# A diffusion-transformer trunk on one NeuronCore: the context's modulation moved from ScalarE to GpSimd

## What is computed

```python
def modulate(x, g, shift, scale):
    return rms_norm(x, g) * (1.0 + scale) + shift

for l in range(DEPTH):                       # DEPTH = 2
    need_ctx = l < DEPTH - 1
    m  = split(silu(c)     @ ada_w[l] + ada_b[l], 6)      # latent:  sh1, sc1, g1, sh2, sc2, g2
    mc = split(silu(c_ctx) @ ada_w[l] + ada_b[l], 6)      # context: csh1, csc1, ...
    h_l = modulate(x,  norm1_g[l], sh1, sc1)
    h_c = modulate(xc, norm1_g[l], csh1, csc1)
    y_c, y_l = mixer_sublayer(h_c, h_l, ...)              # attention, gated DeltaNet, pooling
    x = x + g1 * y_l
    x = x + g2 * expert_choice_ffn(modulate(x, norm2_g[l], sh2, sc2), ...)
    if need_ctx:                                          # layer 0 alone
        xc = xc + cg1 * y_c
        xc = xc + cg2 * expert_choice_ffn(modulate(xc, norm2_g[l], csh2, csc2), ...)
return x
```

## Time and profile before

| | us |
|---|---|
| median of 3 runs | 2088.85 |
| lowest, highest | 2085.29, 2117.83 |
| profiled execution, its own time | 2093.35 |
| its span, first to last instruction | 2091.5 |
| mean granted TensorE clock | 0.968 |

### The profile page before, as it was taken

One profiled execution on the slowest core, in us unless ns is written; L12 is line 12 of the kernel. 1 busy time (PEld: TensorE's weight loads), 2 busy tenths in 40 slices (PEclk: granted clock), 3 DMA queues, 4 the chain that ended last, 5 costly groups with the idle time before them and its releaser, 6 DMA issues.

```text
span 2091.5 us, 41301 instructions
## 1 busy us (share of the span) xinstructions
PE 1957.1 (94%) x17607; PEld 1274.3 (61%) x17607; DVE 725.3 (35%) x1507; ACT 597.9 (29%) x1167; POOL 363.2 (17%) x411
## 2 busy tenths in 40 slices
PE   6999989799999999899999899989889999999998
PEld 4565556678878654455556445546688885455554
DVE  3054233433443316021121325333345443523223
ACT  4111843342232404111110131383342224311111
POOL 2412000143333001211011031200135330000000
PEclk8999999899999999899999999999989999999999
DMA  9400001144444315799999612100100002479996
GB/s 322 134 28 21 21 0 34 37 140 140 160 153 144 100 41 176 232 327 332 344 347 325 241 41 61 41 0 21 51 13 13 18 7 101 161 310 409 414 408 265
DMA packets 196888, 320.65 MB, mean 153 GB/s; under 512 B 10761, under 2 KB 163119, under 8 KB 189583
## 3 DMA queue, kind: packets, MB, share of 16 engines
q1 hardware_dynamic: 184928, 287.20, 39.1%
q0 software_dynamic: 6432, 20.00, 3.5%
q10 hardware_dynamic: 5390, 11.44, 1.6%
HBM read 305.45 MB, written 13.16 MB: 152 GB/s over the span
## 4 chain that ended last, share of the span: by engine, by line
PE 50%; DVE 3%; ACT 3%; issue 2%; DMA 1%; SPq 1%; POOL 0%; DVEq 0%; ACTq 0%; POOLq 0%
PE psum L560 7%; PE psum L1029 6%; PE psum L1077 5%; PE psum L1055 5%; PE psum L1036 3%; PE psum L1140 3%; PE psum L935 3%; PE psum L1089 1%; PE psum L680 1%; PE psum L878 1%; PE psum L866 1%; PE psum L881 1%; PE psum L731 1%; PE psum L700 1%; PE psum L1164 1%
## 5 line engine op out<-in xcount | busy, mean ns | idle before, releaser
L560 PE MATMUL psum<-hT,ring 128*128 128x256 f32 (+2 forms) x976 | 338.9, 504 | 4.7 <-ACT hT L1454 4.2
L560 PEld LDWEIGHTS psum<-hT,ring 128*128 128x128 f32 (+1 forms) x976 | 184.9, 192 | 146.4 <-issue 128.7
L1029 PE MATMUL psum<-ring,arena 128*64 128x256 f32 x1024 | 125.1, 400 | 19.8 <-issue 16.0
L935 PE MATMUL psum<-hT,ring 128*128 128x512 f32 (+1 forms) x384 | 139.6, 521 | 1.1 <-DVE xT L2209 0.9
L878 PE MATMUL psum<-ring,wbuf 64*64 64x64 f32 x1920 | 124.1, 227 | 3.4 <-DVE wbuf L2174 2.8
L881 PE MATMUL psum<-wbuf,ring 64*64 64x64 f32 x1920 | 121.7, 224 | 0.0
L2481 POOL TENSOR_TENSOR mlaw<-ring,lev 128x512 f32<-128x512 f32 x72 | 91.3, 1272 | 162.2 <-PE psum L866 159.9
L1029 PEld LDWEIGHTS psum<-ring,arena 128*64 128x64 f32 x1024 | 78.0, 144 | 60.4 <-issue 29.9
L2296 DVE TENSOR_TENSOR arena<-arena,psum 128x384 f32<-128x384 f32 (+1 forms) x32 | 15.6, 487 | 284.5 <-PE psum L1036 185.4
L935 PEld LDWEIGHTS psum<-hT,ring 128*128 128x128 f32 x384 | 72.6, 190 | 65.3 <-issue 60.3
L878 PEld LDWEIGHTS psum<-ring,wbuf 64*64 64x64 f32 x1920 | 104.1, 141 | 7.0 <-issue 5.0
(11 more groups left out here) (323 smaller groups left out, 3392.8 us busy)
## 6 DMA issues: line engine op xcount, KB each, us to landing
ring<-in_moe_w_gate SPq DMA_DIRECT2D x64, 1024.0 KB, 10.2
ring<-in_ada_w SPq DMA_DIRECT2D x48, 1024.0 KB, 5.3
ring<-in_moe_w_up SPq DMA_DIRECT2D x48, 1024.0 KB, 8.1
ring<-in_moe_w_down SPq DMA_DIRECT2D x32, 1024.0 KB, 10.8
ring<-in_w_in SPq DMA_DIRECT2D x20, 1024.0 KB, 5.9
big<-in_moe_w_down SPq DMA_DIRECT2D x16, 1024.0 KB, 14.4
ring<-in_w_out SPq DMA_DIRECT2D x8, 1024.0 KB, 5.2
xT<-in_moe_w_up SPq DMA_DIRECT2D x8, 1024.0 KB
```

The lines of the kernel that those rows point to most:

```text
L560: m = pe.matmul(b[0:c1 - c0, 0:n], lhsT=w[:, k, c0:c1], rhs=hT[:, k, t0:t0 + n], start=k == 0, stop=k == KD - 1)
L935: m = pe.matmul(b[:, 0:x], lhsT=w[:, k, c:c + P], rhs=mixT[:, k, t0:t0 + x], start=k == OUT_REST[0], stop=k == OUT_GDN[-1])
L1029: m = pe.matmul(b[e * CAP_L:(e + 1) * CAP_L, 0:2 * P], lhsT=xs[:, k, e, 0:CAP_L], rhs=w[e][:, k, :], start=k == 0, stop=k == KD - 1)
```

## The change

ScalarE modulates the latent columns only and counts `h1` or `h2` up for them. The context's columns are modulated in place by GpSimd: a new function `context_norm` waits for the modulation values, then for each block for VectorE's product, and runs one 128x256 `tensor_scalar` with a multiplication and an addition, both with one value for each partition; it counts a new semaphore `hc` up. It is called behind the fill of `big` in both layers, and behind the DeltaNet in layer 0. TensorE waits for `hc` as well as for `h1` and, in layer 0, `h2`. In layer 0 `parameters(0)` now stands behind the eight operations of the first norm, and its own wait is gone.

```diff
@@ TensorE, input projection
                         if key[2] == "pool0":
                             pe.wait_ge(s["h1"], k + 1)
+                            pe.wait_ge(s["hc"], k + 1)
@@ TensorE, router
                     pe.wait_ge(s["h2"], k + 1)
+                    if need_ctx:
+                        pe.wait_ge(s["hc"], KD + k + 1)
@@ ScalarE, norm
                     act.wait_ge(s["hx%d" % which], k + 1)
-                    for g in segs:
-                        t0, n = SEGS[g]
-                        c = 1 - g
-                        m = act.activation(hT[:, k, t0:t0 + n], hT[:, k, t0:t0 + n], ACT.Identity,
-                                           bias=mods_of[l][:, (0 if which == 1 else 3) * KD + k, c:c + 1],
-                                           scale=amod_of[l][:, which - 1, k, c:c + 1])
-                    m.then_inc(s["h%d" % which], 1)
+                    act.activation(hT[:, k, CTX:T], hT[:, k, CTX:T], ACT.Identity,
+                                   bias=mods_of[l][:, (0 if which == 1 else 3) * KD + k, 0:1],
+                                   scale=amod_of[l][:, which - 1, k, 0:1]).then_inc(s["h%d" % which], 1)
@@ GpSimd
+            def context_norm(l, which):
+
+                s = sems[l]
+                pool.wait_ge(s["mods%d" % which], 1)
+                for k in range(KD):
+                    pool.wait_ge(s["hx%d" % which], k + 1)
+                    x = hT[:, k, 0:CTX]
+                    pool.tensor_scalar(x, x, amod_of[l][:, which - 1, k, 1:2],
+                                       mods_of[l][:, (0 if which == 1 else 3) * KD + k, 1:2], ALU.mult, ALU.add
+                                       ).then_inc(s["hc"], 1)
...
                 pool.memset(at(big, 0, (2 * UW,)), 0.0).then_inc(s["upad"], 1)
+                context_norm(l, 1)
                 if l == 0:
-                    evacuated(pool, ("am", ADA_FIRST - 1))
                     parameters(0)
...
+                if need_ctx:
+                    context_norm(l, 2)
                 product_ready(pool, ("rt", l))
```

More of the change, by code:

```diff
@@ L307, in build_program @@
         s_outrow = sem("s_outrow")
-        NAMES = ["zero", "zrow", "pcol", "par", "mods1", "mods2", "rinv", "sq1", "sqd1", "hx1", "h1", "sq2", "sqd2", "hx2", "h2", "upad", "pool", "sqm",
+        NAMES = ["zero", "zrow", "pcol", "par", "mods1", "mods2", "rinv", "sq1", "sqd1", "hx1", "h1", "hc", "sq2", "sqd2", "hx2", "h2", "upad", "pool", "sqm",
                  "abw", "abraw", "abexp", "abln", "gbd", "row1", "rowr", "rowa", "row2", "nm", "pv", "cv1", "qkv", "lsq",
```

## The result

The changed kernel takes **2104.2 us** (median of 22 runs, 2096.14 to 2118.42), the kernel before 2094.0 us beside it (22 runs, 2081.76 to 2117.83). The ratio is 1.0048, 95% interval 1.0032 to 1.0064: 10 us slower, between 6.7 and 13.4. That is within 2% and inside the forecast's range of 2084 to 2111 (its middle was 2094), and about twice the +5.3 us of its sum. The profiled execution took 2109.81 us with a span of 2108.0.

The account below looks back on a forecast made before the run. TensorE, busy 94% of the span, bounds the kernel. Stretches of +4.3 us and 1 for the clock on the profiled 2093.35 give 2098.7; on the median's scale 2088.85 + 5.3 = 2094 us, range 2084 to 2111.

Parts of the forecast that it names:

- The places: Three norms, both of layer 0 and the first of layer 1, hold the possible gain, the largest at layer 1.
- GpSimd's operation, 0.93 us: Each of 24 added GpSimd modulations in the norms was priced at 0.93 us from line 2414, within 0.35 to 1.85.
- The lower bound, 0.35: Lowest price of one GpSimd modulation, 0.35 us, estimated from a plain copy; the three norms would then give -3.1 us.
- the prediction's own formula for pairs: In the norms, 0.82 us for a product after release plus GpSimd's operation less 0.14 hidden: 1.61 for one k.
- The alternation: In the three norms VectorE's products and GpSimd's operations take turns, 1.61 us for one k; 2094 us, chance 0.50.
- rival B: In the norms VectorE keeps the port until all eight products end; 15 to 25 us, time 2104, chance 0.13.
- The sum by stretches: Delays of +0.2 and +1.6 us at layer 0's two norms and +2.5 at layer 1's first, +4.3 together.
- The clock, 1 us within 0 to 5.2: Clock lost through TensorE's pauses at layer 1's first norm, taken as short: 1 us, bounds 0 and 5.2.
- What was costed at nothing: Moved parameter DMAs, the later pooling chain, 24 extra TensorE waits and the load of GpSimd's code: 0 us.
- rival E: GpSimd's code load starts only when layer 0's first context columns are there; sum 12.9 us, time 2103, chance 0.07.
- D: A GpSimd operation in the norms costs 1.85 us; some 25 us at the bound, 2114, middle about 2104, chance 0.15.
- C: GpSimd's single-scalar reads don't block VectorE's products in the norms; -3.3 us, time 2085.6, chance 0.15.

Follow-up runs that it names:

- the three shares: Kernel before with one norm given to GpSimd: layer 0's second +4.2 us, layer 1's first +3.1, layer 0's first with the moved loads +1.7.
- the probe with gaps: Changed kernel plus a tail repeating VectorE products and GpSimd modulations, in this round with a wait between products; the tail adds some 75 us.
- experiment 4: Changed kernel with the inverse roots left in PSUM and each product split at 256 columns; 2087.12 us, ratio 0.9967 to the kernel before.
- experiment 8: Kernel before, ScalarE alone, with the latent columns taken first and signalled apart from the context ones; 2090.77 us, ratio 1.0000.

## Why the prediction was right, and where it was wrong

**The places.** Right as far as the runs can tell: the three shares make 9.0 of 9.4 us, with about 4 us of uncertainty on each. The ranking, layer 1's first norm (+2.5) ahead of the second of layer 0 (+1.6), stays open: the times say 3.1 and 4.2, with intervals that overlap, and the traces 3.6 and 3.0, unless the clock falls in the second norm. The first norm of layer 0 was to lose 0.2 us and lost 1.8 to 2.5.

**GpSimd's operation, 0.93 us.** Wrong: 0.55 to 0.56. The row it was taken from has one operation and costs more than the form with two. The lower bound, 0.35, was nearer. By the prediction's own formula for pairs, 0.82 + (0.56 - 0.14) = 1.24 us, and the probe with gaps shows 1.23; that part of the working holds. The Trainium skill (GPSIMD Engine Reference, Engine selection), which was set aside for the row, has one-input operations roughly line-rate; the prediction put that at its lower bound, 0.35, and the 0.55 measured is nearer to it than to 0.93.

**The alternation, the likeliest case (0.50).** Wrong for this code, and this is the step that failed. The rows it rested on the earlier trace rows show single operations meeting; there the second waits for the first. VectorE's eight products are queued back to back, a new one every 0.87 us while each lasts 0.95, and GpSimd got in only around every third: 2.67 and 2.80 us for an operation of 0.56, while the products grew by 0.20 us twice. The prediction had seen "products start every 0.87 though each lasts 0.95" and booked it under rival B, at 0.13. In its place the runs show something between the two: the second context columns come at +6.6 us, where alternation had 4.2, and the last ones at +10.55. Both cases had the last ones later, alternation at 13.25 and B at about 14.5, but only because they priced the operation at 0.93. At the measured 0.56 alternation would have had them at 1.82 + 0.42 + 6 x 1.24 + 0.56 = +10.2, ahead of the last step of today (10.79), and its sum would have been near nothing. That the forecast had the right sign was luck: the price that was too high made up for a blockade that was too mild. The Trainium skill (SBUF — State Buffer, Who interferes with whom) says that the two contend, and they do; that the second to issue waits for the whole of the first is what the probe with waits shows, not the back-to-back one, where GpSimd waits for three products.

**The sum by stretches.** +0.2, +1.6 and +2.5 were worked out from the *last* columns. What decided was an early block: TensorE's steps of 1.31 us can't catch up from the second one, at +6.78: seven of them took 9.19 us and ended at +15.97, against 804.58 - 791.59 = 12.99, so 3.0 us are lost with the clock at 2.4 GHz. At layer 1, where two products of 0.43 make a step, the last one starts at 6.78 + 6 x 0.86 = 11.9, against 1221.77 - 1210.98 = 10.79: +1.1, and +1.5 was found with the clock up.

**The clock, 1 us within 0 to 5.2.** Too small: 2.6 us where it fell in the second norm of layer 0 and about 2 at layer 1 (15.2 to 15.8 against 13.49). After TensorE's pauses of 2.6 and 1.3 us it fell in one of four traces in the second norm of layer 0, and at layer 1 in all six. "These pauses are short" came from the alternation, and went with it.

**What was costed at nothing.** Right. The parameter loads are issued by 61.4, and the pooling chain starts at 61.38, 0.7 us later than in the earlier trace rows (timeline of the changed kernel); nobody waited for it.

```profile
60.80 0.62 POOL L2386 DMA_DIRECT2D gpar<-in_gdn_dt_bias  x1
61.38 1.58 POOL L2415 TENSOR_TENSOR big<-big 128x799 f32<-128x799 f32 x1
```

The load of GpSimd's code sits behind the fill, 24 us ahead of its first use; rival E is out:

```profile
L2365 POOLq MODIFY_POOL_CONFIG  x2: 8/10/13, 20.3 to 20.3; - x2
```

**The rivals.** D (a dear operation) was wrong in its cause; C's condition, a read that does not block, was false here, but experiment 4 made it true, and its outcome came with it: 2.8 us less in the three stretches, where C had 3.3, and 6.9 in the time. B had its time right, 2104, by a sum that is larger than what happened (15 us at its own low end, +10.0 measured, on a kernel before that took 5 us longer in these runs).

## What to carry to other kernels

Before giving a second engine a share of the work, ask whether both can reach their operands at the same time. Here GpSimd, beside a run of VectorE instructions with two SBUF inputs, got two operations through in seven of VectorE's; with one of these inputs in PSUM it ran at its own pace. Price a shared port for back-to-back instructions from back-to-back rows, not from single meetings, and count the delay of the *second* block, with the consumer's remaining steps behind it, not that of the last. Before pricing an instruction by its nearest row, see that the number of its operations is the same. And compare the granted clocks of the runs before explaining a difference of a few us by a stretch: in experiment 8 the stretches won some 3 us and the time did not show it.

## What the runs showed of the hardware that was not expected

- GpSimd's tensor-scalar on 128x256 with two per-partition scalars and two operations takes 0.55 us, with one scalar and one operation 0.91, on 64 or 128 partitions alike.
- Beside back-to-back VectorE products with two SBUF inputs it takes 2.7 to 2.8 us where the products have 768 columns, 2.0 with 512 and 1.2 with 256; beside products with one PSUM input 0.56. The products pay 0.20 us at the fifth and the eighth.
- With a wait between the products the loss is shared instead: 1.2 to 1.25 us for either engine (the first operation 1.32), 1.23 for the pair, and the eight products need 9.34 us instead of 7.43.
- The longer executions of one kernel are those with the lower mean granted clock, 1.8 us for 0.001 over 212 of them.
- After the same waits TensorE's granted clock was 1.2 GHz for 6.9 us in one execution and 2.4 GHz in the next; where it fell, 28 products of the router took 11.80 us instead of 9.19.
